# A decoder layer on one core: each projection matmul over 512 moving columns issued as two over 256

## The chip, the cores and the metric

The kernel runs on one core of one Trainium2 chip. The metric is device time in microseconds; three runs of the kernel before gave 853.39 to 853.71, median 853.39.

## What is computed

One layer of a hybrid decoder for 256 tokens and a model width of 2048, in float32. The reference, cut to what matters here:

```
h = rms_norm(x, norm_gain)                      # (256, 2048)
aq, ak, av, az, bqkv, bz, bbeta, balpha, gate_a, gate_b = split(h @ w_in)
ya = moba_attention(aq, ak, av) * silu(az)      # 8 heads x 128
bq, bk, bv = split(short_conv(bqkv))
o  = gated_delta_rule(bq, bk, bv, g, beta)      # 8 heads x 128, g and beta from balpha and bbeta
yb = rms_norm(o, dn_norm_gain) * silu(bz)
merged = sigmoid(gate_a) * (ya @ w_branch_a) + sigmoid(gate_b) * (yb @ w_branch_b)
out = rms_norm(x + merged @ w_out, final_norm_gain)
```

Most of the arithmetic is in four projections: `h @ w_in` (2048 by 12304), `ya @ w_branch_a` and `yb @ w_branch_b` (1024 by 2048 each) and `merged @ w_out` (2048 by 2048).

## The kernel before

**Tiles.** The 256 tokens are two tiles t of 128. A weight chunk is 512 columns (`CH`), an output bank `pj[0]` or `pj[1]` holds both token tiles of a chunk, `[128, 2, 512]`. The contraction goes over k tiles of 128 rows. On TensorE the stationary operand of a projection matmul is a 128 by 128 tile of the transposed activations, and the moving operand is 512 columns of weights.

**Precision.** Activations and weights are split in two fp32r parts, `hi` and `lo`. A product is three matmuls that add up in one bank: hi by w_hi (L489), hi by w_lo (L490), lo by w_hi (L491). The first two have the same stationary tile; each of the three loads its own.

**Units.** Work is cut into units of two k tiles (`UK`). SyncE brings a unit's weights into a ring of four slots (`w_raw`), ScalarE rounds them to `w_hi` (L801), VectorE forms `w_lo` (L1035), and TensorE takes them in `unit` (L478 to L498): a wait for `lo_ready`, then for each t and each of the two k tiles the three matmuls, 12 in all. Its last matmul raises `unit_used`, on which ScalarE waits before it writes the slot again. At the end of token tile 0 of a chunk `tile0_done` is raised.

**Order of the program on TensorE.** First the transposes of x and `first_unit` (L500 to L522, matmuls in L516 to L518), then eight heads. A head has 24 units in three chunks: the delta branch's columns, the attention branch's, and a chunk of the gates. Head 0 is written out, heads 1 to 7 are one loop. Behind each token tile of a unit the function `between` puts a step of the small work of the heads, if one stands at that place in a table of steps: transposes, scores, and six rounds of a block inversion (L531 to L611 for the delta branch, also for the head before, L623 to L644 for the attention branch). These are the small groups, of one to seven matmuls over 64, 128 or 256 columns in plain fp32. An fp32 matmul is recorded as two passes. Once, in head 0, `beta_decay_inputs` runs 32 fp32r matmuls over 256 columns with 32 or 16 stationary columns (L654 and L656). Then the two branch projections (4 chunks of 4 units each) and the output projection (4 chunks of 8 units). The last output chunk is not in `unit`: L785 to L787 go over all k for token tile 0 and then for tile 1, so that the final norm of tile 0 can begin earlier.

Of the kernel before, what the change touches and what calls it, by code (L numbers as in the profile page):

```python
# [1 line left out]

# [15 lines left out]
CH = 512  # L33
# [34 lines left out]
def build(nc, x, norm_gain, w_in, conv_w, a_log, dt_bias, dn_norm_gain, w_a, w_b, w_out,  # L68
          final_gain, out):
    ctx = ExitStack()  # L70
    with ctx:
        def sb(name, shape, dt=F32):
            return ctx.enter_context(nc.sbuf_tensor(name, shape, dt))
# [6 lines left out]
        w_hi = sb("w_hi", [P, RING, UK * CH], F32R)  # L80
        w_lo = sb("w_lo", [P, RING, UK * CH], F32R)

        xt_hi = sb("xt_hi", [P, KT, SEQ], F32R)
        xt_lo = sb("xt_lo", [P, KT, SEQ], F32R)
# [26 lines left out]
        half = sb("half", [P, 4])  # L111
# [49 lines left out]
        pj = [ctx.enter_context(nc.psum_tensor(f"pj{i}", [P, T, CH], F32)) for i in range(2)]  # L161
# [78 lines left out]
        def parts(number):  # L240

            spare = number - (FIRST_O + NC * OU - RING)
            if spare < 0:
                return w_hi[:, number % RING, :], w_lo[:, number % RING, :]
            cs = slice(spare % 2 * UK * CH, (spare % 2 + 1) * UK * CH)
            return tuple(m[:, :, :].rearrange("p h t -> p (h t)")[:, cs]
                         for m in ((ya_hi, ya_lo), (yb_hi, yb_lo))[spare // 2])
# [203 lines left out]
        def _(pe):  # L453
            def keep_busy(n):

                for _ in range(n):
                    pe.transpose(pj[1][:, 1, 0:P], ident[:, :], ident[:, :])
# [8 lines left out]
            def turn_x(g):  # L466

                pe.wait_ge(x_landed[g], 16)
                if g == 3:
                    pe.wait_ge(cols_ready, 1)  # L470
                if g >= 4:
                    pe.wait_ge(xt_lo_ready, 2 * (g - 3))
                for q in range(4):
                    k, t = 2 * g + q // 2, q % 2
                    mm = pe.transpose(banks[g % 4][:, q * P:(q + 1) * P], x_sb[:, t, k * P:(k + 1) * P], ident[:, :])
                mm.then_inc(x_turned, 1)

            def unit(slot, number, hi, lo, k0, bank, kt_all, free, between=None):  # L478


                pe.wait_ge(lo_ready, number + 1)
                for t in range(T):
                    if k0 == 0:
                        free(t)
                    for i in range(UK):
                        k = k0 + i
                        tok = slice(t * P, (t + 1) * P)
                        cs = slice(i * CH, (i + 1) * CH)
                        pe.matmul(bank[:, t, :], hi[:, k, tok], w_hi[:, slot, cs], start=(k == 0), stop=False)  # L489
                        pe.matmul(bank[:, t, :], hi[:, k, tok], w_lo[:, slot, cs], start=False, stop=False)  # L490
                        mm = pe.matmul(bank[:, t, :], lo[:, k, tok], w_hi[:, slot, cs], start=False,  # L491
                                       stop=(k == kt_all - 1))
                    if t == T - 1:
                        mm.then_inc(unit_used, 1)
                    elif k == kt_all - 1:
                        mm.then_inc(tile0_done, 1)
                    if between is not None:
                        between(t)  # L498

            def first_unit():  # L500

                keep_busy(4)
                turn_x(0)
                keep_busy(10)
                turn_x(1)
                keep_busy(6)
                for k in range(UK):
                    if k == 0:
                        pe.wait_ge(first_lo, 1)
                    else:  # L510
                        pe.wait_ge(lo_ready, 1)
                    pe.wait_ge(xt_lo_ready, k + 1)
                    for t in range(T):
                        tok = slice(t * P, (t + 1) * P)
                        cs = slice(k * CH, (k + 1) * CH)
                        pe.matmul(pj[0][:, t, :], xt_hi[:, k, tok], w_hi[:, 0, cs], start=(k == 0), stop=False)  # L516
                        pe.matmul(pj[0][:, t, :], xt_hi[:, k, tok], w_lo[:, 0, cs], start=False, stop=False)
                        mm = pe.matmul(pj[0][:, t, :], xt_lo[:, k, tok], w_hi[:, 0, cs], start=False, stop=False)  # L518
                mm.then_inc(unit_used, 1)
                turn_x(2)  # L520
                turn_x(3)
# [152 lines left out]
            def iteration(h, first):  # L674
                for j in range(1 if first else 0, UNITS):
# [16 lines left out]
                    def between(t, j=j):  # L692
# [7 lines left out]
                        if first and s == 2 * XU + 1:  # L700
                            cumulate()

                    unit(j % RING, h * UNITS + j, xt_hi, xt_lo, k0, pj[c % 2], KT, free, between)
                    if first and j + 3 < XU:
                        turn_x(j + 3)
                    if first and j == XU - 2:
                        beta_decay_inputs()

            first_unit()
            iteration(0, True)  # L710
            with pe.Fori(1, H) as h:
                iteration(h, False)

            def branch(c, hi, lo, first_unit, number, dn):

                for j in range(BU):
                    def free(t):
                        if number == 0:
                            pe.wait_ge(gate_ready, T * (H - 1) + t + 1)
                        elif number == 1:  # L720
                            pe.wait_ge(mo_nat_ready, T * H)
                        else:
                            pe.wait_ge(a_gated, T * (number - 2) + t + 1)

                    def between(t, j=j):
                        dn_step(dn + T * j + t + SLOTS, H - 1)

                    if c == 0 and j == BU - 1:
                        pe.wait_ge(ya_lo_ready, H)
                    unit(j % RING, first_unit + c * BU + j, hi, lo, UK * j, pj[number % 2], H, free, between)  # L730
# [17 lines left out]
            for c in range(NC):  # L748
                def free(t, c=c):

                    if c < 2:
                        pe.wait_ge(a_gated, T * (c + 2) + t + 1)
                    else:
                        pe.wait_ge(b_gated, T * (c - 2) + t + 1)
                for j in range(BU):
                    if c == 0 and j == BU - 1:
                        pe.wait_ge(yb_lo_ready, H)
                    unit(j % RING, FIRST_B + c * BU + j, yb_hi, yb_lo, UK * j, pj[c % 2], H, free)
                    if j == 2 and c > 0:
                        turn_merged(c - 1)  # L760
# [15 lines left out]
            for t in range(T):  # L776
                pe.wait_ge(sum_ready, T * (c - 2) + t + 1)
                tok = slice(t * P, (t + 1) * P)
                for k in range(KT):
# [3 lines left out]
                    hi, lo = parts(number)  # L783
                    cs = slice(k % UK * CH, (k % UK + 1) * CH)
                    pe.matmul(pj[c % 2][:, t, :], xt_hi[:, k, tok], hi[:, cs], start=(k == 0), stop=False)  # L785
                    pe.matmul(pj[c % 2][:, t, :], xt_hi[:, k, tok], lo[:, cs], start=False, stop=False)
                    mm = pe.matmul(pj[c % 2][:, t, :], xt_lo[:, k, tok], hi[:, cs], start=False, stop=(k == KT - 1))  # L787
# [589 lines left out]
```

## Time and profile before

| what | value |
|---|---|
| median of 3 runs | 853.39 us |
| profiled execution, first to last instruction (span) | 853.9 us |
| TensorE matmuls: busy, count | 839.8 us (98%), 4199 |
| TensorE loads: busy, count | 704.1 us (82%), 4199 |
| VectorE / ScalarE / GpSimd busy | 474.1 / 431.6 / 112.3 us |
| mean granted TensorE clock | 0.996 |
| read from HBM | 139.72 MB, 166 GB/s over the span |

No time of the profiled execution is listed beside its span, so the span stands for it; it is 0.5 us above the median. PE is TensorE's matmuls and PEld its loads of stationary tiles, which overlap the matmuls. A matmul's duration in a row includes its way through the array, which the next one overlaps, so durations add up to more than the time they take. "Idle before" is time in which the engine ran nothing, with what released it.

### The profile page before, as it was taken

How to read it: one execution, taken by the hardware profiler on the slowest of the kernel's cores; microseconds unless marked ns; L12 is line 12 of the kernel's file. 1: busy time of each engine (PE TensorE's matmuls, PEld its weight loads, DVE VectorE, ACT ScalarE, POOL GpSimd, SP SyncE). 2: the span in 40 equal slices, each digit the busy share in tenths (PEclk: the TensorE clock that was granted, in tenths of full speed). 3: DMA queues.
4: the chain of work that ended last, by engine and by line, in shares of the span. 5: the costliest groups of instructions: out<-in, count | busy, mean ns of one | idle time of the engine just before them, and what ended most of it. 6: DMA issues, size and time to landing. Idle time of an engine off the chain costs nothing.

```text
span 853.9 us, 13041 instructions
## 1 busy us (share of the span) xinstructions
PE 839.8 (98%) x4199; PEld 704.1 (82%) x4199; DVE 474.1 (56%) x705; ACT 431.6 (51%) x714; POOL 112.3 (13%) x163
## 2 busy tenths in 40 slices
PE   8899999999999999999999999999999999999996
PEld 7788888888888888888888888888888888888874
DVE  4666447445743664466447544744664556775563
ACT  4574536544554454365536544654464573444441
POOL 8212001200210040012001200210040000001120
PEclk9999999999999999999999999999999999999999
DMA  8955555564555555655455555645555466668652
GB/s 209 230 141 173 147 151 172 151 170 137 182 147 147 147 172 147 163 155 174 124 162 161 166 150 145 196 127 153 153 182 145 147 188 193 177 206 304 198 166 99
DMA packets 179208, 142.17 MB, mean 166 GB/s; under 512 B 10880, under 2 KB 144240, under 8 KB 179056
## 3 DMA queue, kind: packets, MB, share of 16 engines
q1 hardware_dynamic: 179184, 141.85, 57.2%
q8 instruction: 14, 0.23, 0.1%
q14 instruction: 10, 0.08, 0.0%
HBM read 139.72 MB, written 2.10 MB: 166 GB/s over the span
## 4 chain that ended last, share of the span: by engine, by line
PE 94%; SPq 2%; issue 2%; DVE 1%; DMA 1%; ACT 0%; POOLq 0%; POOL 0%; DVEq 0%; ACTq 0%
PE pj L489 27%; PE pj L491 26%; PE pj L490 26%; PE dn_ps L581 2%; PE dn_ps L588 2%; PE dn_ps L570 1%; PE dn_ps L560 1%; SPq L282 1%; PE dn_ps L545 1%; PE dn_ps L531 1%; PE dn_ps L553 1%; DMA w_raw<-in_w_in_dram 1%; SPq L265 1%; SPq L287 0%; PE mo_ps L539 0%
## 5 line engine op out<-in xcount | busy, mean ns | idle before, releaser
L1035 DVE TENSOR_TENSOR w_lo<-w_raw,w_hi 128x1024 fp32r<-128x1024 f32 x251 | 309.3, 1238 | 246.9 <-ACT w_hi L801 245.5
L489 PE MATMUL pj<-w_hi,xt_hi 128*128 128x512 f32 x860 | 357.8, 416 | 2.9 <-DVE w_lo L1035 2.8
L491 PE MATMUL pj<-w_hi,xt_lo 128*128 128x512 f32 x860 | 337.9, 393 | 0.0
L490 PE MATMUL pj<-w_lo,xt_hi 128*128 128x512 f32 x860 | 336.2, 391 | 0.0
L801 ACT ACTIVATE w_hi<-w_raw 128x1024 fp32r<-128x1024 f32 x251 | 261.3, 1055 | 82.6 <-PE pj L491 64.6
L491 PEld LDWEIGHTS pj<-w_hi,xt_lo 128*128 128x128 f32 x860 | 161.6, 188 | 35.8
L489 PEld LDWEIGHTS pj<-w_hi,xt_hi 128*128 128x128 f32 x860 | 162.4, 189 | 30.1 <-issue 3.5
L490 PEld LDWEIGHTS pj<-w_lo,xt_hi 128*128 128x128 f32 x860 | 162.7, 189 | 27.2
L896 ACT ACTIVATE xs<-dn_ps 128x256 f32<-128x256 f32 x48 | 18.4, 384 | 141.3 <-PE dn_ps L570 141.3
L387 POOL TENSOR_TENSOR ro<-ro,half 128x2 f32<-128x2 f32 x8 | 5.6, 697 | 380.2 <-DVE ro L1205 380.2
L426 POOL TENSOR_TENSOR mt<-lt,levels 128x256 f32<-128x256 f32 x48 | 45.0, 971 | 65.0 <-DVE lt L1178 65.0
L588 PEld LDWEIGHTS dn_ps<-xs,ysb 128*128 128x128 f32 x192 | 28.8, 190 | 4.0
L581 PEld LDWEIGHTS dn_ps<-xs,mt 128*128 128x128 f32 x192 | 28.8, 190 | 3.8
L1139 DVE SCALAR_TENSOR_TENSOR conv<-dn_ps,hs,conv 128x255 f32<-128x255 f32 (+2 forms) x72 | 29.4, 471 | 0.0
L1191 DVE TENSOR_TENSOR xs<-xs,dn_ps 128x128 f32<-128x128 f32 x48 | 13.7, 285 | 27.4 <-PE dn_ps L588 27.4
L446 POOL TENSOR_TENSOR gate<-gate 128x512 f32<-128x512 f32 x6 | 11.2, 1882 | 131.8 <-ACT mt L1015 131.8
L900 ACT ACTIVATE ysb<-dn_ps 128x128 f32<-128x128 f32 x48 | 13.4, 279 | 27.5 <-PE dn_ps L581 27.5
L588 PE MATMUL dn_ps<-xs,ysb 128*128 128x64 f32 x192 | 26.6, 260 | 0.0
L581 PE MATMUL dn_ps<-xs,mt 128*128 128x64 f32 x192 | 26.5, 260 | 0.0
L489 PE MATMUL pj<-w_hi,ya_hi 128*128 128x512 f32 x64 | 26.1, 408 | 0.0
L489 PE MATMUL pj<-w_hi,yb_hi 128*128 128x512 f32 x64 | 25.2, 393 | 0.0
L491 PE MATMUL pj<-w_hi,ya_lo 128*128 128x512 f32 x64 | 25.1, 392 | 0.0
(245 smaller groups left out, 818.5 us busy)
## 6 DMA issues: line engine op xcount, KB each, us to landing
w_raw<-in_w_in_dram SPq DMA_DIRECT2D x384, 256.0 KB, 3.1
w_raw<-in_w_out_dram SPq DMA_DIRECT2D x64, 256.0 KB, 3.7
w_raw<-in_w_branch_a_dram SPq DMA_DIRECT2D x32, 256.0 KB, 3.3
w_raw<-in_w_branch_b_dram SPq DMA_DIRECT2D x32, 256.0 KB, 3.6
gate<-in_x_dram SPq DMA_DIRECT2D x8, 256.0 KB, 5.5
gate<-in_x_dram SPq DMA_DIRECT2D x4, 512.0 KB, 7.5
gate<-in_final_norm_gain_dram SPq DMA_DIRECT2D x1, 1024.0 KB, 8.9
out_dram<-gate SPq DMA_DIRECT2D x1, 768.0 KB, 3.6
```

Source lines behind the costliest of these rows:

```text
L426: pool.tensor_tensor(mt[:, n, :, :], lt[:, :, :], levels[:, n, None, :].to_broadcast([P, T, P]), ALU.mult).then_inc(mt_ready, 1)
L489: pe.matmul(bank[:, t, :], hi[:, k, tok], w_hi[:, slot, cs], start=(k == 0), stop=False)
L490: pe.matmul(bank[:, t, :], hi[:, k, tok], w_lo[:, slot, cs], start=False, stop=False)
L491: mm = pe.matmul(bank[:, t, :], lo[:, k, tok], w_hi[:, slot, cs], start=False, stop=(k == kt_all - 1))
L581: mm = pe.matmul(packed(A, 0, n)[:, t], mt[:, n, t, :], x[:, t], start=True, stop=True)
L588: mm = pe.matmul(packed(B, T, n)[:, t], ysb[:, n, t, :], xT[:, t], start=True, stop=True)
L801: act.activation(w_hi[:, slot, :], w_raw[:, slot, :], ACT.Copy).then_inc(hi_ready, 1)
L896: act.activation(xs[:, 0:T, :].rearrange("p t n -> p (t n)"), B[:, 0:T * P], ACT.Copy).then_inc(xs_ready, 1)
L900: act.activation(halves(ysb[:, n, :, :], n, 0), packed(A, 0, n), ACT.Copy).then_inc(y_ready, 1)
L1035: dve.tensor_tensor(w_lo[:, slot, :], w_raw[:, slot, :], w_hi[:, slot, :].bitcast(F32), ALU.subtract).then_inc(lo_ready, 1)
L1139: dve.scalar_tensor_tensor(out=conv[:, p, back:SEQ], in0=u_[:, 0:SEQ - back], scalar=tap, in1=conv[:, p, back:SEQ], op0=ALU.mult, op1=ALU. ...
L1191: dve.tensor_tensor(xT, xT, packed(B, T, n), ALU.subtract).then_inc(xsT_ready, 1)
```

## The change

In `unit` and in `first_unit` a loop over two halves of the chunk stands around the three matmuls. For each half the three go over 256 of the 512 weight columns into the matching half of the bank. The flag that starts an accumulation is set only on the first half of the first k tile, and the one that ends it only on the second half of the last. The semaphore is raised by the last matmul of the second half. L785 to L787 are left as they are, and nothing on another engine is touched.

```diff
                     for i in range(UK):
                         k = k0 + i
                         tok = slice(t * P, (t + 1) * P)
-                        cs = slice(i * CH, (i + 1) * CH)
-                        pe.matmul(bank[:, t, :], hi[:, k, tok], w_hi[:, slot, cs], start=(k == 0), stop=False)
-                        pe.matmul(bank[:, t, :], hi[:, k, tok], w_lo[:, slot, cs], start=False, stop=False)
-                        mm = pe.matmul(bank[:, t, :], lo[:, k, tok], w_hi[:, slot, cs], start=False,
-                                       stop=(k == kt_all - 1))
+                        last_k = k == kt_all - 1
+                        for half in range(2):
+                            cs = slice(i * CH + half * CH // 2, i * CH + (half + 1) * CH // 2)
+                            o = bank[:, t, half * CH // 2:(half + 1) * CH // 2]
+                            pe.matmul(o, hi[:, k, tok], w_hi[:, slot, cs], start=(k == 0 and half == 0), stop=False)
+                            pe.matmul(o, hi[:, k, tok], w_lo[:, slot, cs], start=False, stop=False)
+                            mm = pe.matmul(o, lo[:, k, tok], w_hi[:, slot, cs], start=False,
+                                           stop=(last_k and half == 1))
                     if t == T - 1:
                         mm.then_inc(unit_used, 1)
```

The same is done to the three matmuls of `first_unit` (L516 to L518).

Order of TensorE at the top of the loop over heads, before, token tile 0 of the first unit and the small group behind it:

```order
364 L489 MATMUL pj<-w_hi,xt_hi 128x512
365 L490 MATMUL pj<-w_lo,xt_hi 128x512
366 L491 MATMUL pj<-w_hi,xt_lo 128x512
367 L489 MATMUL pj<-w_hi,xt_hi 128x512
368 L490 MATMUL pj<-w_lo,xt_hi 128x512
369 L491 MATMUL pj<-w_hi,xt_lo 128x512
370 L585 ISA
371 L588 MATMUL dn_ps<-xs,ysb 128x64 x2
```

The same place in the changed program, the second k tile and the group (lines are 10 lower here):

```order
658 L477 MATMUL pj<-w_hi,xt_hi 128x256
659 L478 MATMUL pj<-w_lo,xt_hi 128x256
660 L479 MATMUL pj<-w_hi,xt_lo 128x256
661 L477 MATMUL pj<-w_hi,xt_hi 128x256
662 L478 MATMUL pj<-w_lo,xt_hi 128x256
663 L479 MATMUL pj<-w_hi,xt_lo 128x256
664 L575 ISA
665 L578 MATMUL dn_ps<-xs,ysb 128x64 x2
```

A k tile of a token tile is now six matmuls instead of three, each of half the width; what stands behind them, and where, is the same.

## Rows read from the trace of the kernel before

**Rows 1.** The page: busy time by engine; chain that ended last, by engine, by line
```profile
PE 839.8 (98%) x4199; PEld 704.1 (82%) x4199; DVE 474.1 (56%) x705; ACT 431.6 (51%) x714; POOL 112.3 (13%) x163
...
PE 94%; SPq 2%; issue 2%; DVE 1%; DMA 1%; ACT 0%; POOLq 0%; POOL 0%; DVEq 0%; ACTq 0%
PE pj L489 27%; PE pj L491 26%; PE pj L490 26%; PE dn_ps L581 2%; PE dn_ps L588 2%; PE dn_ps L570 1%; PE dn_ps L560 1%; SPq L282 1%; PE dn_ps L545 1%; PE dn_ps L531 1%; PE dn_ps L553 1%; DMA w_raw<-in_w_in_dram 1%; SPq L265 1%; SPq L287 0%; PE mo_ps L539 0%
```

**Rows 2.** Groups by line, engine PE: out<-in, shapes, count | busy us, mean ns | idle
```profile
L489 PE MATMUL pj<-w_hi,xt_hi 128*128 128x512 f32 x860 | 357.8, 416 | 2.9 <-DVE w_lo L1035 2.8
...
L489 PE MATMUL pj<-w_hi,ya_hi 128*128 128x512 f32 x64 | 26.1, 408 | 0.0
L489 PE MATMUL pj<-w_hi,yb_hi 128*128 128x512 f32 x64 | 25.2, 393 | 0.0
...
L785 PE MATMUL pj<-w_hi,xt_hi 128*128 128x512 f32 x16 | 6.2, 389 | 0.0
...
L516 PE MATMUL pj<-w_hi,xt_hi 128*128 128x512 f32 x4 | 1.6, 411 | 0.0
```

**Rows 3.** Waits: engine line waited for, us in total, times, longest us
```profile
ACT w_hi L801 <- PE pj L491: 64.6, 45, 1.7
...
PE pj L489 <- DVE w_lo L1035: 2.8, 1, 2.8
```

**Rows 4.** Chain, window 775 to 800: start us, us, what; first and last of 111 pieces
```profile
774.96 0.23 PE pj L489
775.18 0.23 PE pj L490
...
799.89 0.23 PE pj L491
```

**Rows 5.** Chain, window 36 to 41: 32 matmuls over 256 columns, then L489
```profile
37.02 0.12 PE mo_ps L654
37.14 0.12 PE mo_ps L656
...
37.73 0.11 PE mo_ps L654
...
40.67 0.23 PE pj L489
```

**Rows 6.** Groups by line, engine PEld: loads of 128 and of 32 columns
```profile
L489 PEld LDWEIGHTS pj<-w_hi,xt_hi 128*128 128x128 f32 x860 | 162.4, 189 | 30.1 <-issue 3.5
...
L654 PEld LDWEIGHTS mo_ps<-xt_hi,yb_hi 128*32 128x32 f32 x16 | 1.7, 108 | 0.3
```

**Rows 7.** Timeline, window 421.49 to 422.65: start us, us, what (PEld rows are loads)
```profile
421.50 0.55 PE L588 MATMUL dn_ps<-xs,ysb 128*128 128x64 f32 x4
421.50 0.41 PEld L588 LDWEIGHTS dn_ps<-xs,ysb 128*128 128x128 f32 x3
421.83 0.19 PEld L489 LDWEIGHTS pj<-w_hi,xt_hi 128*128 128x128 f32 x1
...
421.95 0.19 PEld L490 LDWEIGHTS pj<-w_lo,xt_hi 128*128 128x128 f32 x1
```

**Rows 8.** Timeline, engine PE, window 420 to 440: five matmuls behind a small group
```profile
420.35 0.39 PE L490 MATMUL pj<-w_lo,xt_hi 128*128 128x512 f32 x1
...
421.27 0.40 PE L491 MATMUL pj<-w_hi,xt_lo 128*128 128x512 f32 x1
```

**Rows 9.** DMA of the whole span: an instruction queue; the issue of a small transfer
```profile
q8 instruction: 14, 0.23, 0.1%
...
convs<-in_norm_gain_dram SPq DMA_DIRECT2D x1, 8.0 KB, 1.7
```

**Rows 10.** DMA, window 200 to 660: all queues that moved anything
```profile
q1 hardware_dynamic: 104343, 72.08, 54.6%
```

**Rows 11.** Busy time by window
```profile
core 0: us, PE busy (x) PEld busy (x) DVE busy (x) ACT busy (x) POOL busy (x), PEclk, DMA share, GB/s
...
500.00:600.00 100.00, 100.00 (x520) 84.44 (x519) 52.45 (x80) 51.16 (x88) 9.60 (x13) 1.00 0.54 154
```

More of the change, by code:

```diff
@@ L514, in first_unit @@
                         tok = slice(t * P, (t + 1) * P)
[L515 to L518, printed above, removed]
+                        for half in range(2):
+                            cs = slice(k * CH + half * CH // 2, k * CH + (half + 1) * CH // 2)
+                            o = pj[0][:, t, half * CH // 2:(half + 1) * CH // 2]
+                            pe.matmul(o, xt_hi[:, k, tok], w_hi[:, 0, cs], start=(k == 0 and half == 0), stop=False)
+                            pe.matmul(o, xt_hi[:, k, tok], w_lo[:, 0, cs], start=False, stop=False)
+                            mm = pe.matmul(o, xt_lo[:, k, tok], w_hi[:, 0, cs], start=False, stop=False)
                 mm.then_inc(unit_used, 1)
```

## The prediction

> **What bounds the kernel now.** I read the page first. TensorE is busy 98% of the span and holds 94% of the chain that ended last, and 79% of the span is the chain's share of three lines alone: L489, L490, L491, the projection matmuls [rows 1]. The list of waits comes second. TensorE waits for data 2.8 us at the largest entry of L489, while ScalarE waits 64.6 us for TensorE [rows 3], so the other engines run ahead and a change of theirs is not felt. In a stretch of 100 us in the middle TensorE is busy for all of it, at a granted clock of 1.00, the 2.4 GHz level, with VectorE and ScalarE near half [rows 11]. So the time is the sum of what each load and matmul pair costs TensorE.
>
> The duration in a group (389 to 416 ns, [rows 2]) is not that cost, since matmuls overlap. I take the distance between starts. In the output projection, where nothing is put between, the first of 111 pieces of the chain starts at 774.96 and the last at 799.89 [rows 4]: 24.93 us / 110 = **226.6 ns** for a load of 128 columns and a matmul over 512. The load has 189 ns in its own row [rows 6] and is wholly inside that distance.
>
> **The change part by part.**
>
> *1. What is split.* L489 runs 860 + 64 + 64 times and L516 4 times [rows 2]: 992, and with the two sister lines of each 2976 matmuls. L785 to L787, the last chunk, stay as they are. So 2976 pairs over 512 columns become 5952 pairs over 256; the columns streamed are the same, and 2976 loads are added. The order of work between units, every semaphore increment and every DMA are as before. The increments sit on the last matmul of the second half, at the same place in time if two halves take what one matmul took.
>
> *2. The stream of a half.* The trace has a row for it: the beta and decay inputs, 32 matmuls over 256 columns of the same kind of data, each with a load of its own. From the seventh on, 37.73 to 40.67 with 26 distances [rows 5], that is 2.94 / 26 = **113.1 ns**. Twice that is 226.2, against 226.6 for the whole. So streaming costs by the column, with nothing left over per matmul that the row could show: term 0.
>
> *3. The load behind a half.* Those 32 matmuls load only 32 or 16 columns, the changed kernel loads 128 each time, so this is the unknown. The nearest row in the other direction is the small fp32 group of L588: matmuls over 64 columns, each behind a load of 128. Its loads start at 421.50 (three of them), 421.83 (L489's) and 421.95 (L490's) [rows 7]: four distances in 0.45 us, **about 112 ns** from load to load, though each is recorded with 190 ns. There the load binds, and it repeats every 112 ns while the matmul before it runs. A half streams for 113.1 ns. So the load just fits: 113.1 is the larger, and the added cost is 0. The margin is one nanosecond, and that is the weak point of this forecast. The bounds: from below 0 (the stream can't be shortened by a load), from above the reading that the 226.6 ns hold a fixed part that goes with a load of 128 columns. 512 columns at 2.4 GHz are 213.3 ns, 13.3 less than measured; if all of it belonged to the load, a half would take 106.7 + 13.3 = 120 ns, 6.9 more than 113.1. The row at 113.1, with small loads, doesn't exclude that. I take 0, because the bare proportion of rows 4 and 5 explains both without a second term.
>
> The Trainium skill has a rule that speaks against the change (TensorE: Matmul & The Clock Gate, Part 3): it lists a load as overlapping matmuls in flight only when it goes to another row group, and these go to the same one. By it each added load would stand in the sum with its full time, the series case below (+333 us); the trace contradicts it, since a load of 189 ns and a matmul over 512 columns fit in 226.6 ns.
>
> *4. Unsettled stretches.* Behind a small group the distances are longer for a while: from L490 at 420.35 to the fifth start after it, L588's at 421.50 [rows 7, 8], it is 1.15 / 5 = 230 ns, 17 ns in all over the settled rate. The rows of 256 columns begin the same way: six distances from 37.02 to 37.73 [rows 5], 118.3 ns each, 31 ns in all. There are about 30 such groups in each of 8 heads. If the stretch keeps its cost: 0. If it costs 31 in place of 17: 240 x 14 ns = +3.4 us. If it vanishes: 240 x 17 = -4 us. I take +1.5, between the first two, as a half has less slack to settle in.
>
> *5. What hides and what doesn't.* The small groups between units are untouched. The first load of a group now has 113 in place of 227 ns of cover, and needs 112: 0. The added instructions have to reach TensorE, and that is a rival below. DVE, ACT and SP do the same work; if TensorE takes longer, their waits grow and nothing follows from it.
>
> Sum: 0 + 0 + 1.5 = +1.5 us. The profiled execution has a span of 853.9 us, 0.5 above the median of the three runs, 853.4, so I put the sum on the median: **854.9 us**, with -4 to +8 as this case's own range (850 to 861), the upper end being 1.1 ns on each of 5952 pairs, the margin of part 3 gone wrong by itself.
>
> **The rivals.**
>
> *Load-limited (0.18), slower.* The load misses its cover: a pair costs not 113.1 but 116 to 120. It decides from the point where load and hand-over take more than 113.1 ns, at every one of the 5952 pairs. Price: 3 x 5952 = +17 us to 6.9 x 5952 = +41 us, 871 to 894. A variant is that the rate never settles because there is no slack, and stays at the 118.3 of part 4: 5.2 x 5952 = +31 us. For it: the one nanosecond of margin, and that no row has loads of 128 columns behind 256 streamed of this kind. Against: loads at 112 in rows 7 without any loss. A sequencer that can't hand over two instructions per 113 ns for long would look the same; 26 pairs at that rate are all that the trace shows.
>
> *Loop that no longer stays fetched (0.13), slower.* The seven later heads are one loop. The whole span has 14 packets on an instruction queue, 0.23 MB, so 16 KB each [rows 9], and from 200 to 660 us, inside the loop, none at all [rows 10]: the body is held somewhere. It grows by 288 pairs, and if it outgrows the place, each turn waits at the jump back. The nearest price is the 1.7 us of a small transfer [rows 9]: 7 x 1.7 = +12 us, 867; nothing if the queued matmuls cover it. The Trainium skill (Runtime: NRT & Kernel Launch, Instruction fetch mechanics) gives TensorE room for 2048 instructions, which the longer body (576 pairs and the small groups) would still fit, but also says that a jump out of a window of two pages of 256 stalls; the trace contradicts the second, since a body of more than 288 pairs turns without a fetch.
>
> *Loads in series (0.02), far slower.* 2976 added loads of 112 ns: +333 us. Rows 4 speak against it.
>
> *Nothing changes (0.05).* The second load of the same tile is dropped, or the halves are joined. L489 and L490 share their stationary tile today and both load it, as the equal counts of matmuls and loads say [rows 1], so dropping is unlikely. Time 853.4.
>
> *Faster* has only the vanishing stretches of part 4, at most 4 us; it is the low end of the forecast.
>
> **How the numbers follow.** My forecast has 0.62. About 0.2% (1.7 us) is what a measurement of this kernel can tell from no change. Of the 0.62, 0.10 lies below -1.7, 0.30 within, 0.22 above. The load-limited case, the series and nearly all of the loop case (0.12 of 0.13) are slower. Faster 0.10; same 0.30 + 0.05 + 0.01 = 0.36; slower 0.22 + 0.18 + 0.12 + 0.02 = 0.54. The predicted time is the likeliest case's. The range is 850 to 880: it takes in the forecast, the loop case and the lower half of the load-limited one, and leaves out 0.09 of that, the series and the tails, some 0.13.
>
> **What would show it.** Right: TensorE's count near 4199 + 2976 = 7175, the distance of two halves of the stretch without small groups 226 to 227 ns, the three lines in about 5950 matmuls over 256 columns with no idle time before them. Load-limited: distances of 116 to 120 there. Loop: instruction packets between 200 and 660 us and a gap at each turn of some 80 us. Wrong altogether: TensorE idle in places where it was not, or a granted clock below 1.00 in the middle.

## The result, and the profile after

The changed kernel takes 885.36 us (median of 4 runs, 885.12 to 886.50) against 853.55 before: a ratio of 1.0363, 95% interval 1.0343 to 1.0383. It is slower by 32 us. The forecast was 854.9 with a range to 880; the time lies outside it.

Some 2 us of this need not be the change. An execution's time is 1.7 to 1.8 us above its span wherever both are recorded, so the profiled execution before (span 853.9) took about 855.6 us, not 853.4, and the two profiled executions differ by 29.5 us. Both have a stretch of 3.4 us, from 28.0 us before and from 25.9 us after, with the granted clock at half, the 1.2 GHz level (0.51 over 28.0 to 31.4 us before). Just ahead of it TensorE had stood idle for 2.8 us before and 2.7 after, at its one long wait for `w_lo`. The profiled execution of e3_tail_split below has the same wait, 2.65 us, and no such stretch, and reaches the beta inputs 2.1 us earlier. The original kernel's times in all later sets are 853.1 to 854.2 us where the granted clock was 0.997 or 0.998, and 854.7 to 856.6 where it was 0.994 to 0.996. It fits that the shorter ones lack the stretch, but only one execution of that kernel has a trace.

The page of the changed kernel, busy time by engine, the instruction queue, the chain by engine, and the first group by line:

```profile
PE 868.9 (98%) x7175; PEld 861.3 (97%) x7175; DVE 473.6 (54%) x705; ACT 433.3 (49%) x714; POOL 111.2 (13%) x163
...
q8 instruction: 23, 0.38, 0.2%
...
PE 94%; SPq 2%; issue 2%; DVE 1%; DMA 1%; ACT 0%; POOLq 0%; POOL 0%; DVEq 0%; ACTq 0%
...
L477 PE MATMUL pj<-w_hi,xt_hi 128*128 128x256 f32 x1720 | 506.8, 295 | 2.7 <-DVE w_lo L1025 2.7
...
L477 PEld LDWEIGHTS pj<-w_hi,xt_hi 128*128 128x128 f32 x1720 | 329.9, 192 | 3.6 <-issue 2.9
```

The bound has not moved: TensorE is busy 98% as before and holds the same 94% of the chain [rows 1], the other engines' busy times are the same to the microsecond or two, and the one wait of the first projection line is 2.7 us where it was 2.8 [rows 3]. The loads are busy 97% in place of 82%. That alone doesn't say that they bind: a load is recorded with 192 ns, and they start every 120 ns. The count grew by 7175 - 4199 = 2976, so nothing was dropped or joined. What changed is the cost of a pair. The chain in the output projection, the stretch that answers to [rows 4], 184 pieces from first to last:

```profile
799.92 0.12 PE pj L477
...
821.88 0.12 PE pj L477
```

183 distances in 21.96 us are **120.0 ns**, in place of the 113.1 that I had put. Two halves take 240 ns where one matmul took 226.6. The starts in the trace are 120 ns apart without a single exception there. The row that I had taken for the stream of a half is still in the changed kernel, with its small loads, right behind halves with loads of 128:

```profile
36.73 0.12 PE pj L479
36.84 0.12 PE mo_ps L644
...
38.13 0.11 PE mo_ps L646
```

It runs at about 113 ns once settled, as in [rows 5]. So the two rates stand side by side in one kernel and at the same width; what differs is the width of the loaded tile, 128 columns against 32 or 16.

Where the 29.5 us of the span (853.9 to 883.4) came from, by the starts of the first matmul of each part in the two traces (8.5 us behind the last matmul are the same in both):

| part | before, us | after, us | difference | 13.3 ns per added load |
|---|---|---|---|---|
| start, to the beta inputs | 36.9 | 36.7 | -0.2 | 84: 1.1 |
| the rest of the eight heads | 624.5 | 645.9 | +21.4 | 2220: 29.6 |
| branch projections | 94.9 | 99.4 | +4.6 | 384: 5.1 |
| output projection, three chunks | 66.2 | 70.0 | +3.8 | 288: 3.8 |
| last chunk, not changed | 23.0 | 22.9 | 0 | 0 |

In the output projection the account closes. In the start, where TensorE waits for x, the added loads don't show. In the heads 8.2 us less were lost than the added loads cost, which the experiments take up.

### The profile page after: what moved, and what is told of

Same layout as the page of the kernel before. It is cut to its first block, busy times and chain, and to the rows that moved or that the text cites. A ratio compares the mean times of both kernels' runs of the same rounds, so it can differ in the third digit from the quotient of the medians.

```text
span 883.4 us, 18993 instructions
## 1 busy us (share of the span) xinstructions
PE 868.9 (98%) x7175; PEld 861.3 (97%) x7175; DVE 473.6 (54%) x705; ACT 433.3 (49%) x714; POOL 111.2 (13%) x163
## 4 chain that ended last, share of the span: by engine, by line
PE 94%; SPq 2%; issue 2%; DVE 1%; DMA 1%; ACT 0%; POOLq 0%; POOL 0%; DVEq 0%; ACTq 0%
PE pj L477 27%; PE pj L479 27%; PE pj L478 27%; PE dn_ps L578 2%; PE dn_ps L571 2%; PE dn_ps L560 1%; PE dn_ps L550 1%; SPq L267 1%; PE dn_ps L543 1%; PE dn_ps L521 1%; PE dn_ps L535 1%; DMA w_raw<-in_w_in_dram 1%; SPq L250 0%; SPq L272 0%; PE dn_ps L584 0%
## 5 line engine op out<-in xcount | busy, mean ns | idle before, releaser
L477 PE MATMUL pj<-w_hi,xt_hi 128*128 128x256 f32 x1720 | 506.8, 295 | 2.7 <-DVE w_lo L1025 2.7
L479 PE MATMUL pj<-w_hi,xt_lo 128*128 128x256 f32 x1720 | 487.5, 283 | 0.0
L478 PE MATMUL pj<-w_lo,xt_hi 128*128 128x256 f32 x1720 | 486.8, 283 | 0.0
L477 PEld LDWEIGHTS pj<-w_hi,xt_hi 128*128 128x128 f32 x1720 | 329.9, 192 | 3.6 <-issue 2.9
L478 PEld LDWEIGHTS pj<-w_lo,xt_hi 128*128 128x128 f32 x1720 | 329.9, 192 | 0.4
L479 PEld LDWEIGHTS pj<-w_hi,xt_lo 128*128 128x128 f32 x1720 | 329.1, 191 | 0.0
L477 PE MATMUL pj<-w_hi,ya_hi 128*128 128x256 f32 x128 | 37.2, 291 | 0.0
L477 PE MATMUL pj<-w_hi,yb_hi 128*128 128x256 f32 x128 | 36.5, 285 | 0.0
L479 PE MATMUL pj<-w_hi,ya_lo 128*128 128x256 f32 x128 | 36.2, 283 | 0.0
L479 PE MATMUL pj<-w_hi,yb_lo 128*128 128x256 f32 x128 | 36.2, 283 | 0.0
L478 PE MATMUL pj<-w_lo,yb_hi 128*128 128x256 f32 x128 | 36.2, 283 | 0.0
L478 PE MATMUL pj<-w_lo,ya_hi 128*128 128x256 f32 x128 | 36.2, 283 | 0.0
```

The source lines that it names most:

```text
L477: pe.matmul(o, hi[:, k, tok], w_hi[:, slot, cs], start=(k == 0 and half == 0), stop=False)
L478: pe.matmul(o, hi[:, k, tok], w_lo[:, slot, cs], start=False, stop=False)
L479: mm = pe.matmul(o, lo[:, k, tok], w_hi[:, slot, cs], start=False, stop=(last_k and half == 1))
```

## The experiments

Theory **F**: with 128 stationary columns of fp32r, a pair takes n / 2.4 ns for its n moving columns and 13.3 ns more in which nothing streams, whatever n is. Theory **L**: streaming costs 0.4427 ns a column as [rows 4] and [rows 5] suggest together, and a load of this kind can't repeat faster than every 120 ns. Both give 226.7 and 120; for other sizes they differ.

**A sweep of sizes.** Behind the last matmul of the kernel before, blocks of 24:

```diff
+            pe.wait_ge(sum_ready, T * (NC - 1))
+            for i in range(24):
+                pe.matmul(pj[0][0:128, 0, 0:512], xt_hi[:, i % KT, 0:128], w_hi[:, 0, 0:512], start=True, stop=True)
+            for i in range(24):
+                pe.matmul(pj[0][0:64, 0, 0:512], xt_hi[:, i % KT, 0:64], w_hi[:, 0, 0:512], start=True, stop=True)
...
```

> Blocks of 24 fp32r matmuls, each with its own load, stand behind the last matmul of the kernel before; the output is the same. Measured are the distances between starts for c stationary and n moving columns. Theory F (a load of 128 columns leaves a fixed part of 13.3 ns in which nothing streams, on top of n / 2.4): 226.7 ns at 128 by 512, 200 at 448, 173.3 at 384, 146.7 at 320, 133.3 at 288, 120 at 256; and with fewer stationary columns less, so 220 or so at 32 by 512. Theory L (streaming costs 0.4427 ns a column, and a load of 128 columns of fp32r can't repeat faster than every 120 ns): 226.7, 198.3, 170.0, 141.7, 127.5 and 120, and 226.7 at 32 by 512 too; with 96 or fewer stationary columns 113.3 at 256 columns. The two differ by 5 ns at 320 and at 6.7 ns at 32 by 512.

The chain of this run: start us, us for the whole block, line, count. In order the blocks have 128, 64, 32, 16 stationary columns at 512 moving; then 128 stationary at 448, 384, 320, 288, 256; then 96, 64, 32, 16 at 256; then 128 at 256 with one and the same tile loaded each time:

```profile
845.08 5.44 PE pj L795 x24
850.52 5.52 PE pj L797 x24
856.04 5.56 PE pj L799 x24
861.60 5.56 PE pj L801 x24
867.16 4.87 PE pj L803 x24
872.03 4.18 PE pj L805 x24
876.22 3.51 PE pj L807 x24
879.73 3.16 PE pj L809 x24
882.89 2.87 PE pj L811 x24
885.76 2.78 PE pj L813 x24
888.54 2.72 PE pj L815 x24
891.26 2.72 PE pj L817 x24
893.98 2.72 PE pj L819 x24
896.71 2.87 PE pj L821 x24
```

Each divided by 24: 384 columns 174 ns (F 173.3, L 170.0), 320 columns 146.3 (F 146.7, L 141.7), 288 columns 131.7 (F 133.3, L 127.5), 256 columns 119.6. **L falls.** 448 columns came to 202.9, 3 above F; the second sweep comes back to this size. With fewer stationary columns at 256 it is 115.8 at 96 and 113.3 at 64, 32 and 16: half of the fixed part is gone. At 512 moving columns F expected it to shrink too (220) and L expected no change (226.7), and it grew instead: 230.0 at 64 and 231.7 at 32 and 16. So F fails there, and the fixed part is not simply a price by the column loaded. With 128 stationary columns it is 12 to 13.3 at five of the six widths and 16 at 448; with fewer it moves between 6.7 and 18.4. The last block, with one and the same tile loaded each time, runs at the same 120.0 once settled.

**A second sweep**, in the same manner, for what the part depends on.

> More blocks behind the last matmul of the kernel before, output the same, to ask what the 13.3 ns beside n / 2.4 depend on, at 128 stationary columns. If on the output bank just written: alternating banks gives 213 and 107 ns at 512 and 256 columns, else 226.7 and 120. If on the rows: 64 rows give less than 120. If on the side that the operands stand on: weights stationary and activations moving differ from 120. If on fp32r: bf16 gives 216 and 109, else 227 and 120. If the load's repeat of 111 to 112 ns is a floor under n / 2.4 + 13.3: 224 columns (106.7) stands at 111 or 112. Alternating 512 and 256 columns: the mean of 226.7 and 120 is 173.3, if the part belongs to each pair.

The chain again. Blocks at 128 stationary columns: 512 and 256 columns into alternating banks; 256 into alternating halves of one bank; 256 with 64 rows; 256 with weights stationary and activations moving; 224, 192, 128 columns; 448 and 480 columns, 60 times; bf16 at 512 and at 256; 512 and 256 in turn; plain fp32 at 256, 12 matmuls recorded as 24 passes:

```profile
843.23 5.44 PE pj L795 x24
848.67 2.87 PE pj L797 x24
851.54 2.88 PE pj L799 x24
854.42 3.06 PE pj L801 x24
857.47 3.04 PE pj L803 x24
860.51 2.67 PE pj L805 x24
863.18 2.66 PE pj L807 x24
865.85 2.65 PE pj L809 x24
868.50 12.45 PE pj L811 x60
880.95 13.00 PE pj L813 x60
893.95 5.20 PE pj L815 x24
899.14 2.62 PE pj L817 x24
901.76 4.17 PE pj L819 x24
905.93 5.18 PE pj L821 x24
```

The bank and the half make no difference (226.7, 119.6, 120.0), and two widths in turn take the mean of both, 173.8 (173.3 expected). The blocks with 64 rows and with swapped operands carry a first distance of 223 ns, whose cause was not looked into; after it 64 rows settle at 120.0 and swapped operands at 118.4. Widths of 224, 192 and 128 all take 111 ns (111.5 settled): that is near the 112 from load to load of [rows 7], and pairs of fp32r go at it too. So neither the repeat of the load nor the handing over of two instructions bounds a half at 120. And **bf16 takes 216.7 and 109.2** (settled 215.8 and 109.1, 2.5 ns over n / 2.4). Plain fp32 takes 215.8 ns for a pass over 256 columns, 2.5 over twice 256 / 2.4. So of the three types only fp32r has the 13.3 ns. The settled distances at 448 and 480 are 206.7 and 216.7, that is 20 and 16.7 over n / 2.4: the part isn't one constant over all widths. Nor is it one constant for a width: at 448 the first sweep had distances of 199 to 207 ns in a repeating order, 202.7 in the mean, and the second had 206.7 for 60 matmuls. The Trainium skill (TensorE: Matmul & The Clock Gate, Part 1) gives n / 2.4 + 2.5 ns for a warm matmul; the bf16 rows agree, and the fp32r rows, with five times that addition, don't; for fp32r the measurement decides.

One question the sweeps leave open. Every matmul in every run has a load of its own, so they can't say whether the fixed part goes with the load or with the matmul, and "per added load" below means per added pair.

The two traces of before and after show one more condition of it. In the stretch at half clock (granted clock 0.5, the 1.2 GHz level) that both have near the start, the timeline of TensorE has before, from the second matmul of it on:

```profile
28.39 0.63 PE L490 MATMUL pj<-w_lo,xt_hi 128*128 128x512 f32 x1
...
30.09 0.63 PE L491 MATMUL pj<-w_hi,xt_lo 128*128 128x512 f32 x1
```

and after:

```profile
26.53 0.41 PE L478 MATMUL pj<-w_lo,xt_hi 128*128 128x256 f32 x1
...
29.09 0.37 PE L478 MATMUL pj<-w_lo,xt_hi 128*128 128x256 f32 x1
```

Four distances before are 426.7 ns each and twelve after are 213.3, which is n / 1.2 for 512 and 256 columns with nothing over it. So at half clock two halves take exactly what one matmul takes: the forecast's term of 0 holds there, and the fixed part of fp32r shows at the full clock alone.

**Both halves of a tile in a row.** The changed kernel, with the halves inside the three products:

```diff
-                        for half in range(2):
...
+                        for part, (a, b) in enumerate(((hi, w_hi), (hi, w_lo), (lo, w_hi))):
+                            for half in range(2):
...
+                                mm = pe.matmul(o, a[:, k, tok], b[:, slot, cs],
```

> The changed kernel, with the two halves of each stationary tile issued one behind the other, so that each second load brings the tile that was loaded just before. F and L: every load counts, whatever it brings, so 885 us as the change. Rival (the tile is seen to be there, or the 120 ns come from three matmuls in a row adding to the same half bank): 855 to 865 us.

Measured: 885.82 us, ratio 1.0364 (1.0348 to 1.0380), the same as the change. Loading the tile that is already there is not cheaper, and neither the order of the halves nor adding three times to the same half matters.

**The split outside the heads alone.** The split of `unit` is switched on behind the loop over heads:

```diff
+                        split = not in_head[0]
+                        for half in range(2 if split else 1):
...
+            in_head[0] = False
```

> Split in the two branch projections and three chunks of the output projection alone: 672 of the 2976 matmuls, and nothing in the heads. F and L: 672 x 2 x 6.67 ns = +9.0 us, less some 0.5 for small groups in the branch stretch: 862 us. Rival (the loss is made in the heads, by the loop or by the small groups): within 2 us of the kernel before.

Measured: 862.56 against 854.81 on the same chip, ratio 1.0092 (1.0077 to 1.0108), or 7.9 us. By parts +4.5 us in the branches and +3.8 in the output projection, as in the changed kernel. The loss is made in straight code as well, at the same price, so it doesn't need the loop.

**One product of three.** Only the matmul of hi by w_lo is split:

```diff
-                        pe.matmul(bank[:, t, :], hi[:, k, tok], w_lo[:, slot, cs], start=False, stop=False)
+                        for half in range(2):
+                            c2 = slice(i * CH + half * CH // 2, i * CH + (half + 1) * CH // 2)
+                            pe.matmul(bank[:, t, half * CH // 2:(half + 1) * CH // 2], hi[:, k, tok],
+                                      w_lo[:, slot, c2], start=False, stop=False)
```

> The kernel before, with only the second of the three matmuls (hi by w_lo) split in two: 992 added loads in place of 2976. Theory F, a fixed part per load: a third of the steady loss, 992 x 13.3 ns = +13.2 us, less at most 3 us at small groups: 864 to 867 us, and 1.28 us in the stretch of the output projection (96 of them). Rival, that the loss needs an unbroken row of short pairs (the load can't keep up for long, but catches up behind a matmul over 512 columns): within 3 us of before.

Measured: 864.44 us, ratio 1.0116 (1.0100 to 1.0133), about 9.9 us for 992 added loads. In the output projection a set of three products with one split takes 233 + 231 + 113 + 119 = 696 ns for 680 before, 16 more rather than 13.3. In the heads it adds 7.4 us for 740 loads, 10 ns each. The loss needs no unbroken row of short pairs; each added load brings its own, a little more where widths alternate.

**Uneven pieces.** The changed kernel with 320 and 192 columns:

```diff
-                            cs = slice(i * CH + half * CH // 2, i * CH + (half + 1) * CH // 2)
+                            a, b = (0, 320) if half == 0 else (320, CH)
+                            cs = slice(i * CH + a, i * CH + b)
```

> The changed kernel, with the 512 columns cut into 320 and 192 in place of 256 and 256: the same count of loads and of columns. Rule from the sweeps: a pair takes n / 2.4 + 13.3 ns, but not under the 111.5 ns from load to load. So 146.7 + 111.5 = 258.2 ns for two pieces, 31.5 more than one matmul over 512, 2976 times: +93.7 us, less some 8 at small groups as in the change: 936 to 950 us. Theory L (0.4427 ns a column, 120 ns floor) gives 141.7 + 120 = 261.7, +104 us, 946 to 960. A cost per load alone, without a floor (93.3 ns for 192 columns) gives 240, as the change: 885.

Measured: 938.31 us, ratio 1.0980 (1.0952 to 1.1009), +84.7 us, inside the rule's 936 to 950 and outside L's. The chain of the output projection, each line of three now in two forms:

```profile
850.50 0.17 PE pj L478
...
851.28 0.17 PE pj L478
```

From one L478 to the same place six pairs later it is 0.78 us (0.776 by the starts), 259 ns for two pieces; the rule gave 258.2. The rule, fixed part plus stream, but not under the load's 111.5, holds for an arrangement on which it was not made. It holds for the pair of pieces; in this stretch the single distances go from 85 to 169 ns.

**What the small groups gave back.** The 8.2 us in the heads. The chain behind a group of L588 of the kernel before, and the same step of the program after:

```profile
428.30 0.39 PE dn_ps L588 x4
428.69 0.28 PE pj L489
428.98 0.23 PE pj L490
...
430.13 0.22 PE dn_ps L570 x2
```

```profile
434.52 0.39 PE dn_ps L578 x4
434.91 0.17 PE pj L477
435.08 0.12 PE pj L478
435.20 0.12 PE pj L479
```

Before: from 428.98 to 430.13 five matmuls take 1.15 us, 230 ns each: they run unsettled until the next group breaks in. After: within 6 ns of 120 from the second on, a little under it in the mean. Over the loop (202 groups before and 201 after), the time of a group and its surroundings above 226.7 or 120.0 ns per projection distance is 521 ns before and 487 after: 34 ns less. Of these, 27 are the later matmuls (+21 ns a group before, -6 after), 10 the matmuls at the edges, and the group itself takes 3 more. 34 ns x 29 groups x 8 heads = 7.9 us, the missing account. To see whether that can be had without the rest, only the first matmul behind a group is split:

```diff
+                        if i == 0 and fresh[0]:
+                            for half in range(2):
...
+                        fresh[0] = False
```

> The kernel before, with only the first projection matmul behind each small group split in two, some 250 of 2976. In the changed kernel a group costs TensorE some 35 ns less than before. If that comes from the first matmul behind it (edge and unsettled stretch), this gives up 13.3 ns and gains up to 35: 848 to 852 us. If it comes from all the matmuls between two groups being short, only the 13.3 ns are left: 250 x 13.3 = +3 us, 857 us.

Measured: 855.26 against 854.81, ratio 1.0002 (0.9992 to 1.0011). Neither case came: the 13.3 ns of the added load are made good, and nothing is left over. In its trace the two halves behind a group take 202 and 118 ns where one matmul took 314, and the matmuls over 512 columns behind them still take 224 to 238. So most of what the halves gave back (27 of the 34 ns) comes from all the matmuls between two groups being short, where each costs 13.3 ns to have.

**A cheaper type for the small products.** Since bf16 has almost no fixed part, the two small products are taken on the upper 16 bits of the same data, with a step of two, in the unsplit kernel. This leaves out the lower bits of these two products.

```diff
+            def upper(m):
+                return m.bitcast(mybir.dt.bfloat16).rearrange("p (n e) -> p n e", e=2)[:, :, 1]
...
+                        pe.matmul(bank[:, t, :], upper(hi[:, k, tok]), upper(w_lo[:, slot, cs]), start=False, stop=False)
```

> The kernel before, unsplit, with the two small products of each three (hi by w_lo, lo by w_hi) taken on the upper 16 bits of the same fp32r data as bf16, read with a step of two; it drops the lower bits of these two terms. The sweep had 215.8 ns for bf16 over 512 against 226.7 for fp32r. If the 13.3 ns belong to the type: 2044 matmuls x 10.9 ns = 22 us faster, 831 us. If the stepped read costs what an fp32r read costs: within 2 us of before. If the step halves the stream: 2044 x 200 ns more, above 1200 us.

Measured: 868.82, ratio 1.0169 (1.0148 to 1.0189), none of the three. The timeline, matmuls and loads, of the output projection:

```profile
779.58 0.59 PE L492 MATMUL pj<-w_hi,xt_hi 128*128 128x512 f32 x1
...
780.00 0.10 PEld L493 LDWEIGHTS pj<-w_lo,xt_hi 128*128 128x128 bf16 x1 [0.27 <-issue]
780.01 0.40 PE L493 MATMUL pj<-w_lo,xt_hi 128*128 128x512 bf16 x1
780.02 0.10 PEld L494 LDWEIGHTS pj<-w_hi,xt_lo 128*128 128x128 bf16 x1
```

L493's load does not start beside the fp32r matmul in front of it, at 779.58, but 0.42 us later, after idle time with no releaser ("issue"). The matmul of L493 follows at once, and L494's load starts beside it. The three products take 704 ns, 46 more than 226.7 + 2 x 215.8 = 658. I put all of the 46 on the turn from fp32r to bf16 and back; the next run shows that a part of it was something else. In it the products of a unit are sorted by type:

```diff
+                    full = [(i, 0) for i in range(UK)]
+                    small = [(i, part) for i in range(UK) for part in (1, 2)]
+                    order = full + small if t == 0 else small + full
```

> The run before it, with the products of a unit sorted by type: fp32r, fp32r and four bf16 for token tile 0, four bf16 and two fp32r for token tile 1, so one turn to bf16 and one back per unit instead of four. A turn and back cost 704 - (226.7 + 2 x 215.8) = 46 ns in the run before, in which the three matmuls of a k tile took 704 ns in place of 680. If 46 ns stand per turn and back and a stepped bf16 read streams at 215.8: per unit 8 x 10.9 - 46 = 41 ns gained, 248 units, 10 us faster, 843 us. If a stepped read streams no faster than fp32r (226.7): 248 x 46 ns = 11 us slower, 865 us.

Measured: 852.49 against 855.10 in the same set of runs, ratio **0.9970 (0.9959 to 0.9980)**, 0.3% faster and the only version that beats both kernels, with the small products at lower precision. It came between the two forecasts, 843 and 865. The stepped bf16 matmuls in the timeline of this run, TensorE alone, output projection:

```profile
780.51 0.39 PE L499 MATMUL pj<-w_hi,xt_lo 128*128 128x512 bf16 x1
...
781.64 0.39 PE L499 MATMUL pj<-w_lo,xt_hi 128*128 128x512 bf16 x1
```

Five distances from 780.51 to 781.64 are 225 ns each by the starts, not the 215.8 of the sweep where the data lay side by side. With 225 for a stepped matmul the 46 ns come apart: 2 x 9 for the step, and 704 - (226.7 + 2 x 225) = 27 for the turn. In this run a unit of the output projection takes 2740 ns for 4 fp32r and 8 bf16 matmuls, which leaves 33 for the one turn, and it is 20 more than the 2720 before. So the branch and output projections gain nothing (95.0 and 66.7 us for 94.9 and 66.2); the gain is in the heads, 621.2 us for 624.5. It is to be looked for behind the small groups. Of 195 groups in the loop 121 are followed by a bf16 matmul, and there it is 337 ns from the group's last start to the second start behind it, where the kernel before has 370 in the mean. The rest of the gain was not added up. The start is no part of it: the profiled execution of this version is 1.7 us earlier at the beta inputs, but it has no stretch at half clock. A copy in bf16 without the step would have to be made by some engine and wasn't tried.

## Why the prediction was wrong, point by point

- *What bounds the kernel* was right: the same shares of the chain, TensorE without waits, and the time followed the pairs.
- *Part 1, the counts*, was right: 7175 matmuls, 2976 loads added.
- *Parts 2 and 3 failed, and part 3's choice is the step.* Part 2 read twice 113.1 ns out of the beta inputs and concluded that streaming costs by the column, with nothing per matmul. That agreement of 226.2 with 226.6 was an accident of two different additions: 13.3 ns at 512 columns with 128 loaded, 6.7 at 256 with 32 or 16 loaded. Part 3 had the right value as its upper bound, 106.7 + 13.3 = 120 ns, and the forecast took the lower end, "because the bare proportion of rows 4 and 5 explains both without a second term". The row taken as nearest differed from the change in the stationary columns, and the first sweep shows that this counts: 120.0 at 128, 113.3 at 32 and 16. The size of the step: at 120 in place of 113.3 ns, 5952 x 6.67 ns = 39.7 us where the sum had 0; less the 8.2 of the heads, 1.3 in the start and 0.5 in the branches that is the 29.6 of the parts within the rounding. That the upper bound was exactly the value is in part luck, since its reason, that the whole fixed part belongs to a load of 128 columns, did not hold: with 16 columns loaded half of it was left at 256 moving columns, and more than all of it at 512.
- *Part 3's load.* That a load of 128 columns repeats every 112 ns was right (111 in the second sweep, for fp32r too), and the margin of a nanosecond was not what gave way.
- *Part 4, unsettled stretches*, had the wrong sign: +1.5 us put, about -8 measured, twice the -4 that it allowed for a stretch that vanishes. Halves are near 120 ns from the second distance on, and the first six distances of the beta inputs were no model for them.
- *The base.* The sum was put on 853.4 us as if the profiled execution were 0.5 us above it; that execution took about 855.6 us. This moves the forecast by 2 us and decides nothing.
- *The rivals.* Load-limited, at 0.18 with 871 to 894 us, was the case that came, by its upper price per pair (6.9 ns for 6.67), though not by its mechanism: the load keeps up (111.5 ns), and so does the handing over; the fixed part is what is paid twice. Its price left out what the small groups give back, and the range cut it in half at 880. The variant of a rate that never settles, 118.3 ns, did not come either: it settled, at 120. The loop stayed fetched: there are 23 packets of instructions over the span in place of 14, but in the window of 200 to 660 us of the changed kernel, as in [rows 10], the DMA view has one queue alone:

```profile
q1 hardware_dynamic: 104370, 70.09, 53.3%
```

Loads in series and a change that does nothing fell with the count and the 120 ns.
- *The range* was wrong where it left out the upper half of a rival whose mechanism was written down, with its number, as a bound of the unknown.

## What to carry to other kernels

Read a pair's cost at two widths with the same stationary tile before saying that it goes by the column: two rows that differ in the load as well can agree by accident. Here an fp32r matmul with 128 stationary columns and a load of its own paid 13.3 ns beside n / 2.4 at 512, 384, 320 and 256 columns, and about 111 ns in all at 224 and less. So cutting the moving side in two cost 13.3 ns a cut, 3.6% of this kernel, and 9.8% where one piece fell under the 111 ns. Where a bound of an unknown has an arithmetic reason (here the 13.3 ns over the clock), the range has to hold it whole.

## What the runs showed of the hardware that was not expected

- fp32r differs from bf16 and plain fp32 in the fixed part: 13.3 ns against 2.5 at 512 columns of bf16, and 2.5 for a pass of plain fp32 over 256.
- The fixed part of fp32r is not monotone: 13.3 at 512 columns, 16.7 at 480, 16 in one sweep and 20 in the other at 448, 13.3 at 384; fewer stationary columns lower it at 256 (6.7 at 64 or fewer) and raise it at 512 (16 to 18). Six of the settled distances (113.3, 120, 146.7, 173.3, 206.7, 226.7) are whole multiples of 6.67 ns, 16 periods of 2.4 GHz; those at 480 and 288 columns (216.7 and 132.0) are not. At half clock there is none: 426.7 ns at 512 columns and 213.3 at 256. What makes the fixed part, no run settles.
- After a group of plain fp32 matmuls, fp32r matmuls over 512 columns run at about 230 ns for up to nine of them before they settle at 226.7; halves don't.
- A bf16 load behind an fp32r matmul was not taken ahead; a turn to bf16 and back cost some 27 to 33 ns. A bf16 operand read with a step of two took 225 ns over 512 columns in place of 215.8.
